# MoE expert passes on one Trainium2 core: thirteen pass widths, weights stationary in halves of 64 columns, down's output turned by VectorE

## The reference

```python
logits = h @ w_router + b_router                      # (1024, 32)
top_val, top_idx = lax.top_k(logits, 4)
gates = softmax(top_val)
# for every expert e and its rows xb:
gu = xb @ w_gu[e] + b_gu[e]                           # 1024 -> 2048
gate = minimum(gu[:, :1024], 7.0); up = clip(gu[:, 1024:], -7.0, 7.0)
act = gate * sigmoid(1.702 * gate) * (up + 1.0)
y = act @ w_dn[e] + b_dn[e]                           # 1024 -> 1024
x = x + sum of gate * y over a row's 4 experts
```

## Time and profile before

| | us |
|---|---|
| median of three runs (2326.01 to 2326.75) | 2326.26 |
| span of the profiled execution, first to last instruction | 2307.6 |
| TensorE busy in it | 2250.9 |
| VectorE busy | 955.8 |
| ScalarE busy | 423.4 |
| GpSimd busy | 606.0 |
| expert passes (first to last matmul) | 615.56 to 2144.40 |

### The profile page before, as it was taken

How to read it: one execution, slowest core, us unless ns; L and a number is a source line. 1 busy time by engine, 2 the same in 40 slices (tenths; PEclk the granted TensorE clock), 3 DMA queues, 4 the chain that set the end, 5 groups by cost and what they waited for, 6 DMA issues and landing times.

```text
span 2307.6 us, 40594 instructions
## 1 busy us (share of the span) xinstructions
PE 2250.9 (98%) x15298; PEld 1579.7 (68%) x15298; DVE 955.8 (41%) x2112; ACT 423.4 (18%) x873; POOL 606.0 (26%) x915
## 2 busy tenths in 40 slices
PE   8999999998799999999999999999999999999998
PEld 5555466454455578878878788778887887777443
DVE  4664477245634333434434434323333222222464
ACT  3110265302311111111111111011111100010344
POOL 0555587100232321121121121222121111111320
PEclk9999999998899999999999999999999999999999
DMA  5100111421599999888898899878887666642540
GB/s 197 42 25 6 42 38 45 167 72 51 221 398 410 398 410 360 320 323 327 316 328 321 318 326 333 290 275 311 319 319 299 248 238 240 221 174 117 203 164 37
DMA packets 103093, 533.51 MB, mean 231 GB/s; under 512 B 22522, under 2 KB 26410, under 8 KB 50930
## 3 DMA queue, kind: packets, MB, share of 16 engines
q1 hardware_dynamic: 76754, 465.57, 53.8%
q0 software_dynamic: 26272, 67.02, 8.3%
HBM read 498.02 MB, written 31.23 MB: 229 GB/s over the span
## 4 chain that ended last, share of the span: by engine, by line
PE 86%; DMA 5%; DVE 4%; ACT 3%; issue 1%; POOL 1%; SPq 0%; POOLq 0%; ACTq 0%; DVEq 0%
PE ps L1890 38%; PE ps L1903 16%; PE ps L1658 5%; DMA wg<-in_w_gu 4%; PE ps L1950 3%; PE ps L1647 2%; PE ps L1768 2%; PE ps L1763 2%; PE ps L1928 2%; DVE x L1507 2%; PE ps L1609 1%; PE ps L1677 1%; PE ps L2031 1%; PE ps L1743 1%; PE ps L1711 1%
## 5 line engine op out<-in xcount | busy, mean ns | idle before, releaser
L1890 PEld LDWEIGHTS ps<-xT,wg 128*128 128x128 f32 x6912 | 872.7, 191 | 20.0 <-issue 13.4
L1890 PE MATMUL ps<-xT,wg 128*128 128x128 f32 (+4 forms) x6912 | 882.4, 290 | 0.0
L1494 DVE TENSOR_SCALAR gb<-ps,bcur 128x256 f32<-128x256 f32 x216 | 104.5, 484 | 820.4 <-PE ps L1890 820.4
L1903 PE MATMUL ps<-wd,actT 128*128 128x512 f32 x864 | 375.4, 592 | 0.0
L1903 PEld LDWEIGHTS ps<-wd,actT 128*128 128x128 f32 x864 | 162.5, 190 | 193.8 <-issue 187.3
L920 ACT ACTIVATE sg<-gb 128x256 f32<-128x256 f32 x216 | 90.0, 417 | 774.7 <-DVE gb L1494 774.7
L606 POOL DMA_INDIRECT xg<-normalised_rows,rowc x184 | 177.9, 967 | 74.1 <-issue 45.1
L637 POOL COPY rowc<-rowq 128x8 uint32 (+1 forms) x34 | 6.3, 187 | 563.9 <-DVE xT L1447 563.9
L1950 PE MATMUL ps<-wg,xT 128*32 128x256 f32 x2304 | 134.5, 386 | 11.7 <-DVE xT L1447 8.4
L655 POOL DMA_DIRECT2D bin__182<-in_b_exp x33 | 18.9, 574 | 412.0 <-issue 285.1
L2031 PE MATMUL ps<-wpg,xnT 128*128 128x512 f32 x256 | 112.9, 595 | 6.1 <-ACT xnT L932 6.1
(11 more groups left out here) (411 smaller groups left out, 2349.5 us busy)
## 6 DMA issues: line engine op xcount, KB each, us to landing
wg<-in_w_gu SPq DMA_DIRECT2D x264, 1024.0 KB, 6.9
wd<-in_w_dn SPq DMA_DIRECT2D x132, 1024.0 KB, 6.6
expert_rows<-yb POOLq DMA_DIRECT2D x48, 256.0 KB, 8.5
expert_rows<-yb POOLq DMA_DIRECT2D x60, 128.0 KB, 4.6
hT<-in_x_cm SPq DMA_DIRECT2D x8, 512.0 KB, 9.1
cumb<-gate_sums SPq DMA_DIRECT2D x4, 1024.0 KB, 4.7
x<-in_x_tm SPq DMA_DIRECT2D x1, 4096.0 KB, 13.7
wout<-in_w_out SPq DMA_DIRECT2D x1, 4096.0 KB, 20.9
```

The lines of the kernel that those rows point to most:

```text
L1494: v.tensor_scalar(gb[:, f % 2, :], ps[:, f % 2, 0:W], bcur[:, f:f + 1], 7.0, ALU.add, ALU.min).then_inc(S("g_ready"), 1)
L1890: ins = m.matmul(ps[:, f % 2, g_ * W:g_ * W + w], wg[:, f, k, g_, :], xT[:, k, 0:w], start=(k == 0), stop=(k == KT - 1))
L1903: ins = m.matmul(ps[:, 2 + c, :], actT[:, f, 0:P], wd[:, c, f, :], start=(f == 0), stop=(f == FT - 1))
```

## The change

The widths become thirteen, 64 to 240, run in an order that mixes narrow and wide (`RUN`). There is one kind of pass. In both products the weights stand still and the rows move. For widths up to 128 the 128 weight columns are split in two halves of 64, one after the other in program order, each into its own 64 partitions of the same bank. Down loops over f outermost; its output has the model's columns in partitions and rows along the bank, so VectorE turns it in 32 x 32 blocks from PSUM to `yb` (`turn_out`, two operations of 1024) behind the input turns and the waits for `y_free` and `dn_mm`. ScalarE's copies, the narrow pass with its turned activations, and `bias_rows` are gone. The down weights and their chunks are laid out anew (same sizes). The width tables are made by whole-table comparisons. The stores write pieces of 256 columns.

```diff
-WIDTHS = (96, 128, 144, 192, 224, 256)
+WIDTHS = (64, 80, 96, 104, 112, 120, 128, 136, 144, 176, 192, 208, 240)
+NW = len(WIDTHS)
+WMAX = WIDTHS[-1]
+SPLITS = -(-T // WMAX)
+RUN = (128, 64, 240, 80, 208, 96, 192, 104, 176, 112, 144, 120, 136)
...
+                sp.dma_start(wd[:, 2 * j:2 * j + 2], w_dn[bass.ds(e, 1), j].rearrange("o p f m -> (o p) f m")).then_inc(S(f"dn_ld{j}"), 16)
...
                 wait_at("y_evac", b + 2)
+                with pool.If(n > P):
+                    for r in range(4):
+                        pool.dma_start(ys[bass.ds(r0, W), 256 * r:256 * r + 256].rearrange("(c j) d -> j c d", j=32),
+                                       yb[32 * r:32 * r + 32, :, :, :].rearrange("j a c d -> j (a c) d")).then_inc(S("y_st"), 16)
+                with pool.Else():
+                    for r in range(4):
+                        pool.dma_start(ys[bass.ds(r0, P), 256 * r:256 * r + 256].rearrange("(c j) d -> j c d", j=32),
+                                       yb[32 * r:32 * r + 32, 0, :, :]).then_inc(S("y_st"), 16)
...
+            with act.Fori(0, npass) as b:
+                for f in range(FT):
+                    act.wait_ge(S("g_ready"), b * FT + f + 1)
+                    a.activation(sg[:, f % 2, :], gb[:, f % 2, :], ACT.Sigmoid, scale=1.702).then_inc(S("sig_ready"), 1)
...
+            dve.wait_ge(S("hs_st"), 16 * 6)
+            for i, w in enumerate(RUN):
                 v.memset(cwid[:, i, :], float(w))
+                v.memset(cnext[:, i, :], float(max((x for x in WIDTHS if x < w), default=0)))
...
+            for i in range(1, SPLITS):
+                link(v.scalar_tensor_tensor(R(2), R(0), float(WMAX * i), R(2), ALU.is_gt, ALU.add))
+            v.tensor_tensor(e32(cown), e32(cwid), each(2), ALU.mult)
+            link(v.tensor_tensor(e32(cbase), e32(cnext), each(2), ALU.mult))
+            v.tensor_tensor(e32(cown), e32(cown), each(0), ALU.is_ge)
+            link(v.tensor_tensor(e32(cbase), e32(cbase), each(0), ALU.is_lt))
+            link(v.tensor_tensor(e32(cmask), e32(cown), e32(cbase), ALU.mult))
+            v.tensor_tensor(e32(cend), e32(cmask), e32(cwid), ALU.mult)
+            v.tensor_tensor(e32(crow), e32(cmask), each(0), ALU.mult)
+            link(v.tensor_tensor(e32(cnum), e32(cmask), each(2), ALU.mult))
+            v.tensor_reduce(R(11), e32(cend).rearrange("p c e -> p e c"), AX_X, ALU.add)
...
+            def turn_out(half):
+                return v.transpose(yb[:, half, :, :].rearrange("p c (o i) -> p c o i", i=32),
+                                   ps[:, 2:6, :].rearrange("p b (x h c j) -> p h c (b x) j", x=2, h=2, c=4)[:, half])
...
                 turn_in(0)
                 turn_in(1).then_inc(S("xt_evac"), 1)
+                dve.wait_ge(S("y_free"), b + 1)
+                dve.wait_ge(S("dn_mm"), b * 4 + 4)
+                turn_out(0)
+                turn_out(1).then_inc(S("y_evac"), 1)
...
             def expert_pass(b, w):
+                cols = 64 if w <= P else P
                 pe.wait_ge(S("xt_evac"), b + 1)
                 for f in range(FT):
                     pe.wait_ge(S(f"in_ld{f}"), b * 16 + 48)
                     pe.wait_ge(S("gu_evac"), b * FT + f + 1)
                     for g_ in range(2):
                         for k in range(KT):
-                            ins = m.matmul(ps[:, f % 2, g_ * W:g_ * W + w], wg[:, f, k, g_, :], xT[:, k, 0:w], start=(k == 0), stop=(k == KT - 1))
+                            for h in range(0, P, cols):
+                                ins = m.matmul(ps[h:h + cols, f % 2, g_ * W:g_ * W + w], wg[:, f, k, g_, h:h + cols], xT[:, k, 0:w],
+                                               start=(k == 0), stop=(k == KT - 1))
                     ins.then_inc(S("gu_mm"), 1)
                 pe.wait_ge(S("y_evac"), b + 1)
+                for f in range(FT):
+                    if f % 2 == 0:
+                        pe.wait_ge(S(f"dn_ld{f // 2}"), b * 16 + 16)
+                    pe.wait_ge(S("act_ready"), b * FT + f + 1)
+                    for o_ in range(8):
+                        for h in range(0, P, cols):
+                            ins = m.matmul(ps[h:h + cols, 2 + o_ // 2, W * (o_ % 2):W * (o_ % 2) + w], wd[:, f, P * o_ + h:P * o_ + h + cols],
+                                           actT[:, f, 0:w], start=(f == 0 and o_ % 2 == 0), stop=(f == FT - 1), skip_group_check=True)
+                    if f % 2:
+                        ins.then_inc(S("dn_mm"), 1)
+            for c, w in enumerate(RUN):
                 with pe.Fori(ends[c - 1] if c else 0, ends[c]) as b:
+                    expert_pass(b, w)
```

252 lines of the change are left out of this document (23 added, 229 removed).

## The result

The changed kernel takes 2349.75 us (2346.91 to 2359.79, four runs), the kernel before 2326.14 beside it: ratio 1.0113 (1.0092 to 1.0134), 1.1% slower. Forecast were 2205.4. The profiled execution took 2350.32 us with a span of 2348.8.

A forecast was written before the change was run, and what follows sets the result against it. Weight transfers bound the first 209 us of the passes, TensorE's instruction stream the other 1320. Span 2307.6 - 137.3 + 2.7 + 4 + 7.2 + 2.5 = 2186.7, plus 18.7, gives 2205.4 us; own range 2190 to 2225, with rival B 2188 to 2255.

The forecast's parts named there:

- the pace of a pair: Narrow expert passes: two 64-column halves take 0.833w + 2.5 ns at w rows, floor 58.3; 384 pairs a pass.
- -137.3 us: Expert passes: matmul time summed over all 33 passes, 1391.5 us against 1528.8 before.
- 1391.5 + 2.7 + 4: Expert passes: matmul sum, plus 2.7 us for the first pass's half-speed clock, plus 4 us of weight waits.
- the price of a column: TensorE weight loads: a load costs its columns over 1.2 GHz, whatever the rows; the trace's 54 ns for 64 columns agrees.
- Rival A's first form: Narrow passes: a pair's two loads share one port, so passes up to 128 rows cost 42.0 us; 2344 us; A's chance 0.13.
- Rival A's second form: Narrow passes: the queue can't feed four instructions faster than 27 ns each; same 2344 us; A's chance 0.13.
- the 18.7 us: Whole kernel: runs' median 2326.26 us lies 18.7 above the profiled span, added to the forecast span of 2186.7.
- rival B: Passes of 64, 80 and 96 rows: weights bind again at 34.28 us a pass, +39; 2240 us; chance 0.12.
- Routing +7.2: VectorE ahead of the passes: larger tables delay the copy of the row numbers by 7.2 us, ends 4 and 9.
- weights +4: Expert passes: waits for weights, around the two 64-row passes, add 4 us, ends 0 and 13.
- turn_out at nothing: VectorE between passes: two turns from PSUM, 2.6 us together, hidden behind the next pass's first two chunks; taken as 0.
- 2.5 forecast: Tail: later turns after the last matmul and projection weights meeting the stores add 2.5 us, ends 0 and 6.

The follow-up runs named there:

- e2: Changed kernel with the 120-row loop placed ahead of the 144-row loop; with the stall 2305.21 us, 0.9925 of the kernel before.
- e5: Changed kernel with plain row loads (row selection left out) and the 120-row loop ahead of the 144-row loop; without the stall 2208.66 us, 0.9573 of the kernel before.
- e3: Changed kernel with rows of all passes but the first fetched by plain instead of indirect DMAs; 2257.53 us, 0.9716 of the kernel before.
- e10: The kernel before, unaltered, run for its trace in a call with the stall; 2328.23 us, span 2326.7.
- e7: e2 with the second four gathers of every pass left out, rows beyond 128 not fetched; without the stall 2207.87 us, 0.9564 of the kernel before.
- e8: Changed kernel with 80 more waits on TensorE, moving its loops by 40 instructions; without the stall 2278.28 us, 0.9878 of the kernel before.
- e13: e7 again, in another call without the stall; 2209.67 us, 0.9573 of the kernel before.
- e1: Changed kernel with halves in gate/up alone, down loading 128 columns at a time; with the stall 2279.82 us, 0.9812 of the kernel before.
- e15: e6 again, in another call without the stall; 2253.52 us, 0.9782 of the kernel before.
- e17: e2 with the passes' gathers fetching 256 bytes a row instead of 1 KB; with the stall 2316.99 us, 0.9957 of the kernel before.
- e9: The changed kernel, unaltered, in the third call, with the stall; 2345.42 us, 1.0074 of the kernel before.
- e16: The changed kernel, unaltered, in the fifth call, with the stall; 2347.47 us, 1.0086 of the kernel before.
- e4: Changed kernel with the halves undone, 128 columns a weight load everywhere; with the stall 2405.43 us, 1.0348 of the kernel before.
- e6: e1 with each loop's last pass loaded just ahead of that loop on TensorE; without the stall 2260.51 us, 0.9787 of the kernel before.
- e11: e6 with halves in down for 64 and 80 rows and 24 waits moving the loops by 12 instructions; with the stall 2283.44 us, 0.9815 of the kernel before.

## Why the prediction was wrong, point by point

The step that failed is the one from the pace of a pair to the time of a pass. The sum let every narrow pass cost 384 pairs at their pace and put the supply of twice as many instructions at nothing. The runs showed some 96 us of stalls beside the indirect gathers and 45 of a loop whose code is fetched again, and the change of -137.3 us in the passes became +25.6.

**Where 156 us came from.** The passes were to take 1391.5 + 2.7 + 4 = 1398.2 us; they ran from 627.03 to 2181.46, 1554.4. The same stretch takes 1509.8 in e2, so the refetched loop is 44.6; it takes 1413.3 in e5, so the gathers are 96.5 (89.6 in passes of up to 128 rows, the rest in wide ones; e2 and e5 are from calls of both kinds, but within the first call e3 gives 93.2 for the same step); and 15.1 are left. Against the bare 1391.5 they are 21.8, nearly all in first iterations of narrow loops: in e5 the first 64-row pass takes 33.3 us and the second 22.5, the 80-row pass 34.0 for 26.6, the first 96-row pass 34.0 for 31.7. TensorE's waits there are for "issue" (15.7 us from 700 to 985), and the first pass of each narrow loop fetches 5 or 6 blocks; that the one is for the other is argued, not tested.

**The pace of a pair held.** 95.8 ns at 112 rows, 102.5 at 120; the second 64-row pass 22.55 us in e5 with a pair forecast of 58.3 ns (22.4). Loads of 64 columns last 137 ns each and two run side by side. A load of 128 lasts 191, so the price of a column that the prediction quotes fits the difference of 54 ns and not a load's whole length. Rival A's first form, one port for both, is excluded. The rule of the Trainium skill (TensorE: Matmul & The Clock Gate, Part 3, What overlaps) that a load overlaps only where row groups differ does not hold here either, now with fewer moving than stationary columns as well. The wide widths came out to 0.2 us without the stall (77.96 at 240 rows, 57.48 at 176, 47.04 at 144 and 44.48 at 136 in e5); in the changed kernel's trace some passes of 136 and 144 take up to 1.7 more.

**Failed: the rival that was written off.** Rival A's second form said that the queue can't feed four instructions faster than 27 ns each, and I weighed it by L1711 alone, a line with no gather beside it. In general the queue does feed one per 24 ns, and per 14.6 at 64 rows. Beside an indirect gather it does not: five matmuls with their loads in 0.73 us are 73 ns an instruction. The forecast had no term for what an engine that issues nothing to TensorE can do to its instruction supply. Which part of the supply is held up stays open; since no block moves in these stalls, it is not the fetch from memory. The kernel before asks for one per 56 ns and seems to lose 18 us to it (e10), but not in the trace that I had. That rival A's 2344 us lies near the measured time is luck: its equal passes of 42 us aren't there, they take 24 to 58.

**Failed: the 18.7 us.** I read the difference between median and span, 2326.26 - 2307.6, as what lies around the span. The span of every later execution is 1.5 or 1.6 us under its own time (2350.32 and 2348.8; 2328.23 and 2326.7). The other 17 us are the difference between the two kinds of calls: the profile of before fits one without the stall, the median one with it. It was in sight that such a gap is odd, and I explained it away. Without the stall the sum gives 2186.7 + 1.5 = 2188; e5 and e7, with the 120-row loop in its earlier place, measure 2208. That this is near the forecast's 2205.4 is luck: 17 us too many in the offset stand beside 20 that the sum lacks.

**Failed: rival B, by its size.** "Fetching the code of 13 loop bodies while DMA is full" was there, put at no more than 39 us and at the wrong place. First iterations cost some 20 (e5); a body that is fetched again in every pass costs 45, with a DMA share of 0.65 to 0.87 in such passes.

**Routing +7.2 and weights +4.** The copy stands at 608.32, as reckoned. Left out were the register loads on TensorE, which follow the bias products in its queue: 13 in place of 6 put the first matmul at 627.03 for 622.8, 4.3 us before rounding. Each takes 0.64 us of the queue in the trace. The prediction counted what the edit adds on VectorE operation by operation, and on TensorE's own queue not at all. No wait for a weight shows in the passes; 4 was too much.

**turn_out at nothing held**: 1229 ns for a forecast of 1.3, and passes without a gap in e5. The tail ends 167.3 us after the last matmul, 4.1 more than before, for 2.5 forecast.

The sum: 2186.7 + 156.2 + 4.3 + 1.6 = 2348.8.

**The change in a call without the stall** was never timed as it stands. e8, which has one other loop in the bad place, is 1.2% faster than the kernel before there, and e7 and e13 are 4.4 and 4.3% faster, with part of the gathers left out. I take from it that the sign of this change depends on the kind of call; what makes the kind is open. Of the complete versions e1 beats both kernels with the stall (0.9812) and e15, the same with its register loads apart, beats the kernel before without it (0.9782); neither was timed in the other kind of call.

## What to carry to other kernels

Splitting a matmul to shorten it doubles the instructions: ask what the queue must deliver per instruction (here 24 ns), what else is running then, and how many 16 KB blocks the loop's body is, for a body near the limit may be fetched again in every pass by where it happens to lie. In a trace both show as waits for "issue" with no line behind them and in lengthened matmuls; the refetched body shows as packets of the instruction queue besides, the stall beside the gathers does not. And where a median and a profiled span are further apart than other executions put them, the profile may be from other conditions than the time.

## What the runs showed of the hardware

- Beside indirect DMAs issued by GpSimd, TensorE gets an instruction per some 73 ns, with gaps of about 1 us, while no block of code is being fetched. Plain DMAs of the same size on the same queue don't do this (e3); 256 bytes a row do it as 1 KB does (e17). In two of six calls nothing of it was there, on chips that showed it in another call.
- A loop of 1554 TensorE instructions (6.07 blocks) runs from what is kept, or is fetched again pass by pass (36 blocks more over five passes, 123 against 87; 5 to 12 us lost in each), by where it lies (e2, e8). Two further runs of the changed kernel fetched 27 more, not 36 (e9, e16). Loops of 1298 instructions never were fetched again (e1).
- With 64 moving rows behind 128-column loads the granted clock, once it had fallen behind short waits (1.4 us together), stayed at the lower level for 85.3 us without another gap (e4). In e6's profiled execution it fell behind waits of 2.06 and 2.33 us and stayed low for 34.1 us; in e15's, the same kernel, it held.
- A register load on TensorE took 0.64 us of its queue's time: 3.9 to 6.4 us between the turned rows and the first matmul with 13 of them, 0.2 with one (e6, e11, e15).
